# Gating the last weights on GpSimd and closing the last product in two pieces, in a fused two-block transformer kernel

## The reference, cut to what matters

```python
def swiglu(h, w_gate, w_up, w_down):
    return (jax.nn.silu(h @ w_gate) * (h @ w_up)) @ w_down
...
    h = rms_norm(x, g_ffn[l]) * (1.0 + sc_f) + sh_f
    x = x + g_f * swiglu(h, w_ffn_gate[l], w_ffn_up[l], w_ffn_down[l])
    return rms_norm(x, g_final)
```

## Time and profile before

| what | value |
|---|---|
| median of three executions | 961.36 us |
| the profiled execution, its own time | 960.98 us |
| its span, first to last instruction | 959.2 us |
| PE, DVE, ACT, POOL busy | 99%, 72%, 54%, 6% |
| mean granted TensorE clock | 0.997 of full speed |

### The profile page before, as it was taken

The page is one execution under the profiler, slowest core; times in us unless marked ns, Lnnn a source line. Parts: engine busy times, 40 slices in busy tenths (PEclk is TensorE's granted clock), DMA queues, the critical chain, the costliest instruction groups (busy, mean ns, idle before and its releaser), DMA issues.

```text
span 959.2 us, 12959 instructions
## 1 busy us (share of the span) xinstructions
PE 945.3 (99%) x5054; PEld 810.4 (84%) x5054; DVE 685.8 (72%) x932; ACT 518.3 (54%) x732; POOL 54.6 (6%) x96
## 2 busy tenths in 40 slices
PE   8999999999999999999999999998999999999996
PEld 8889888888888888888788888887988888888885
DVE  6956578658888775975788777668678886556555
ACT  6756563536655555264275555547465575444543
POOL 0000121001000002100100000002100000000000
PEclk9999999999999999999999999999999999999998
DMA  9975275527988886183289898764631565655521
GB/s 322 337 253 176 88 268 204 209 88 256 338 278 294 283 295 204 52 314 125 88 317 333 271 306 288 249 221 131 229 132 45 176 225 192 219 176 191 178 71 45
DMA packets 110028, 203.00 MB, mean 212 GB/s; under 512 B 4188, under 2 KB 76144, under 8 KB 106640
## 3 DMA queue, kind: packets, MB, share of 16 engines
q1 hardware_dynamic: 106656, 189.67, 58.4%
q0 software_dynamic: 3168, 12.24, 3.7%
q10 hardware_dynamic: 144, 0.26, 0.1%
HBM read 201.09 MB, written 1.06 MB: 211 GB/s over the span
## 4 chain that ended last, share of the span: by engine, by line
PE 90%; DVE 6%; ACT 2%; issue 1%; POOL 0%; DMA 0%; POOLq 0%; SPq 0%; DVEq 0%; ACTq 0%
PE WB L360 20%; PE YB L385 11%; PE YB L378 10%; PE YB L393 10%; PE WB L363 10%; PE YB L439 4%; PE WB L378 2%; PE WB L342 2%; PE WB L385 2%; PE WB L393 2%; PE WB L349 2%; PE WB L345 2%; PE WB L694 1%; PE WB L713 1%; PE WB L477 1%
## 5 line engine op out<-in xcount | busy, mean ns | idle before, releaser
L1709 DVE TENSOR_TENSOR wl<-raw,wh 128x2048 fp32r<-128x2048 f32 (+1 forms) x146 | 334.3, 2297 | 117.4 <-ACT wh L1101 115.1
L1101 ACT CAST wh<-raw 128x2048 fp32r<-128x2048 f32 (+1 forms) x150 | 285.2, 1905 | 30.5 <-PE YB L439 8.9
L360 PE MATMUL WB<-XS,wh 128*128 128x512 f32 x832 | 208.1, 392 | 0.0
L360 PEld LDWEIGHTS WB<-XS,wh 128*128 128x128 f32 x832 | 152.2, 188 | 29.1
L363 PEld LDWEIGHTS WB<-XS,wl 128*128 128x128 f32 x832 | 113.5, 190 | 8.2
L363 PE MATMUL WB<-XS,wl 128*128 128x256 f32 x832 | 116.0, 282 | 0.0
L378 PE MATMUL YB<-wh,FHT 128*128 128x512 f32 x352 | 109.0, 391 | 0.0
L385 PE MATMUL YB<-wl,FHT 128*128 128x512 f32 x352 | 108.6, 390 | 0.0
L393 PE MATMUL YB<-wh,FLT 128*128 128x512 f32 x352 | 108.5, 389 | 0.0
L1275 ACT COPY U<-WB 128x256 f32<-128x256 f32 x102 | 33.0, 376 | 132.8 <-PE WB L363 132.8
L385 PEld LDWEIGHTS YB<-wl,FHT 128*128 128x128 f32 x352 | 66.1, 188 | 14.1
(11 more groups left out here) (338 smaller groups left out, 1205.2 us busy)
## 6 DMA issues: line engine op xcount, KB each, us to landing
raw<-in_mlp_w SPq DMA_DIRECT2D x64, 1024.0 KB, 5.2
raw<-in_w_ada_t SPq DMA_DIRECT2D x24, 1024.0 KB, 5.1
raw<-in_mlstm_w_in SPq DMA_DIRECT2D x11, 1024.0 KB, 8.0
raw<-in_w_ffn_down SPq DMA_DIRECT2D x11, 1024.0 KB, 4.9
raw<-in_w_ffn_gate SPq DMA_DIRECT2D x10, 1024.0 KB, 5.4
raw<-in_w_ffn_up SPq DMA_DIRECT2D x10, 1024.0 KB, 5.6
raw<-in_mem_w_kv SPq DMA_DIRECT2D x8, 1024.0 KB, 5.1
raw<-in_xattn_wq SPq DMA_DIRECT2D x8, 1024.0 KB, 7.2
```

What stands on the lines that cost most here:

```text
L360: e.matmul(W[:, :], H[:, at(k)], XS[:, k, :], start=k == 0, stop=False)
L1101: f = e.copy(w[:, 0:a * b], raw[:, 0:a * b])
L1709: f = e.tensor_tensor(L[:, 0:a * b], raw[:, 0:a * b], H[:, 0:a * b].bitcast(F32), ALU.subtract)
```

## The change

Three edits go together.

1. POOL multiplies the second 512 columns of both blocks of every down chunk by the gate vector, in place in `raw` (two instructions of 128 x 512 per chunk, 11 chunks). It begins after the norm's last low part (`dve_ln["lo", "ffn", 1, 3]`). ACT's cast of a down chunk waits for POOL and no longer for the landing. DVE then adds the h=1 banks straight to `X`, without the multiplication.
2. The last 512 columns of t=1 come from PE as two pieces: the products of down 9 and 10 for columns 512 to 767 go on in `YB[3]`, those for 768 to 1023 start anew in `YB[0]`. DVE adds all of `YB[3]` to `X` after the first piece and `YB[0]` after the second.
3. ACT squares only columns 512 to 767 of the last half. DVE squares and sums 768 to 1023 itself, adds its sum to POOL's partial one, and makes the last output in one instruction from `X`, the factor and the gain.

```diff
+                        c0, c1 = stops[nb - 1] if nb else 0, stops[nb]
+                        o, start = YB[2 * t + nb] if nb < 2 else apart, (first or nb == 2) and n == 0
+                        if nb == 2 and n == 0:
+                            e.wait_ge(*apart_free)
...
-                    e.wait_ge(*landed(n))
+                    e.wait_ge(*(w_gated[n] if name[0] == "down" else landed(n)))
...
-            for h in range(2):
-                e.wait_ge(*dve_ffn["gated", 1, h])
-                rms_half("out", 1, h)
+            e.wait_ge(*dve_ffn["gated", 1, 0])
+            rms_half("out", 1, 0)
+            e.wait_ge(*dve_ffn["gated", 1, 1])
+            e.activation(JX["out"][1][:, 512:768], X[:, 1, 512:768], ACT.Square, scale=1 / 32,
+                         accum_out=cols(("rms", "out", 1), 6)[:, 1:2]).then_inc(act_ln.add(("ms", "out", 1, 1)))
...
+                if rows == "down" and h == 1:
+                    e.tensor_tensor(X[:, t, cs], X[:, t, cs], YB[2 * t + h][:, :], ALU.add).then_inc(cnt.add(("gated", t, h)))
+                    return
...
+            e.wait_ge(*pe_rows["down", 1, 1])
+            e.tensor_tensor(X[:, 1, 512:1024], X[:, 1, 512:1024], YB[3][:, :], ALU.add).then_inc(dve_ffn.add(("gated", 1, 1)))
             by_g(1, 0)
-            gated("down", dve_ffn, 1, 1, 1)
-            by_g(1, 1)
+            w, last = cols(("rms", "out", 1), 6), X[:, 1, 768:1024]
+            e.wait_ge(*pe_rows["down", 1, 2])
+            e.wait_ge(*dve_ffn["gated", 1, 1])
+            step(e.tensor_tensor(last, last, YB[0][:, 0:256], ALU.add))
+            step(e.scalar_tensor_tensor(U[:, 1, 768:1024], last, 1 / 1024, last, ALU.mult, ALU.mult, accum_out=w[:, 4:5]))
+            e.wait_ge(*po_ln["part", "out", 1])
+            e.tensor_tensor(w[:, 5:6], w[:, 4:5], w[:, 2:3], ALU.add).then_inc(dve_ffn.add("ms"))
             e.wait_ge(*po_ln["r", "out", 1])
-            e.tensor_scalar(U[:, 1, 512:1024], U[:, 1, 512:1024], cols(("rms", "out", 1), 4)[:, 3:4], None, ALU.mult
+            e.scalar_tensor_tensor(U[:, 1, 512:1024], X[:, 1, 512:1024], w[:, 3:4], BV[gi][:, 512:1024], ALU.mult, ALU.mult
...
+            e.wait_ge(*dve_ln["lo", "ffn", 1, 3])
+            for j in range(11):
+                n = N["down", j]
+                r = RAW[n % NR][:, :].rearrange("p (k c) -> p k c", k=2)
+                e.wait_ge(*landed(n))
+                for k in range(2):
+                    f = e.tensor_tensor(r[:, k, 512:1024], r[:, k, 512:1024], GB[:, 1, 512:1024], ALU.mult)
+                f.then_inc(w_gated.add(n))
+            rms_stats("out", (0,))
+            w = cols(("rms", "out", 1), 6)
+            e.wait_ge(*act_ln["ms", "out", 1, 1])
+            e.tensor_scalar(w[:, 2:3], w[:, 1:2], w[:, 0:1], EPS, ALU.add, ALU.add).then_inc(po_ln.add(("part", "out", 1)))
+            e.wait_ge(*dve_ffn["ms"])
+            rsqrt(w[:, 3:4], w[:, 5:6], po_ln.add(("r", "out", 1)))
```

More of the change, by code:

```diff
@@ L305, in build_program @@
         d_bv = [sem(f"in_bv{n}") for n in range(2)]
-        w_hi, w_lo, w_hi0, w_lo0, w_ada, w_pool = (count(n) for n in "w_hi w_lo w_hi0 w_lo0 w_ada w_pool".split())
+        w_hi, w_lo, w_hi0, w_lo0, w_ada, w_pool, w_gated = (
+            count(n) for n in "w_hi w_lo w_hi0 w_lo0 w_ada w_pool w_gated".split())
         pe_turn, pe_front, pe_mlstm, pe_rows, pe_xa, pe_mlp, pe_pool, pe_mix, pe_ffn = (
@@ L399, in tm, with rows @@
                 return parts_[1]()
-            def rows(stage, j, names, xs, first, last, free=None, amid=None, ts=(0, 1)):
+            def rows(stage, j, names, xs, first, last, free=None, amid=None, ts=(0, 1), stops_1=(512, 1024),
+                     apart=None, apart_free=None):
                 ms = [M[n] for n in names]
                 for t in ts:
-                    order = [(nb, n) for nb in range(2) for n in range(len(ms))]
+                    stops = stops_1 if t else (512, 1024)
+                    order = [(nb, n) for nb in range(len(stops)) for n in range(len(ms))]
                     if t == 0:
@@ L414, in rows @@
                             amid()
-                        f = tm(m, 2, 1024, 512 * nb, 512 * nb + 512, YB[2 * t + nb][:, :], t, k0,
-                               first and n == 0, last and n == len(ms) - 1, xh, xl,
+                        c0, c1 = stops[nb - 1] if nb else 0, stops[nb]
+                        o, start = YB[2 * t + nb] if nb < 2 else apart, (first or nb == 2) and n == 0
+                        if nb == 2 and n == 0:
+                            e.wait_ge(*apart_free)
+                        f = tm(m, 2, 1024, c0, c1, o[:, 0:c1 - c0], t, k0,
+                               start, last and n == len(ms) - 1, xh, xl,
                                hi and nb == 0 and (lambda k: hi(t, k)), lo and nb == 0 and (lambda k: lo(t, k)))
@@ L419, in rows @@
                             f.then_inc(pe_rows.add((stage, t, nb)))
-                        elif last and t == nb == 1:
+                        elif last and t == 1 and nb == len(stops) - 1:
                             f.then_inc(pe_rows.add((stage, "end", n)))
@@ L426, in rows @@
                 for n, m in enumerate(ms):
-                    done = (1, 1) if n == len(ms) - 1 else ("end", n)
+                    done = (1, len(stops) - 1) if n == len(ms) - 1 else ("end", n)
                     ends[m] = pe_rows[(stage,) + done if last else (stage, j)]
@@ L1065, in down @@
                        lambda t, k, n=n: hidden(dve_ffn, n, k)) for n in js], js[0] == 0, js[-1] == 10,
-                     free if js[0] == 0 else None)
+                     free if js[0] == 0 else None, stops_1=(512, 768, 1024) if js[-1] == 10 else (512, 1024),
+                     apart=YB[0], apart_free=dve_ffn["gated", 0, 0])
             pair("ffn", [("gate", 0), ("up", 0)], pe_ffn, lambda n: dve_mix["gated", 0, n])
@@ L1401, in rms_half @@
                 cs = slice(512 * h, 512 * h + 512)
-                e.activation(JX[s][t][:, cs], X[:, t, cs], ACT.Square, scale=1 / 32, accum_out=cols(("rms", s, t), 4)[:, h:h + 1]
+                e.activation(JX[s][t][:, cs], X[:, t, cs], ACT.Square, scale=1 / 32, accum_out=cols(("rms", s, t), 6 if s == "out" else 4)[:, h:h + 1]
                              ).then_inc(act_ln.add(("ms", s, t, h)))
@@ L1651, in scalar @@
                 e.copy(FH[0][:, fs], SU[0][:, fs]).then_inc(act_ffn.add(("h", 10, f)))
-            r = [cols(("rms", "out", t), 4)[:, 3:4] for t in range(2)]
+            r = [cols(("rms", "out", t), 6)[:, 3:4] for t in range(2)]
             for h in range(2):
@@ L1664, in scalar @@
             f.then_inc(act_ffn.add(("out", 0)))
-            for h in range(2):
-                e.wait_ge(*dve_ffn["gated", 1, h])
-                rms_half("out", 1, h)
+            e.wait_ge(*dve_ffn["gated", 1, 0])
[3 more added lines that the diff above has]
+                         accum_out=cols(("rms", "out", 1), 6)[:, 1:2]).then_inc(act_ln.add(("ms", "out", 1, 1)))
+            e.wait_ge(*dve_ffn["g", 1, 0])
             e.wait_ge(*po_ln["r", "out", 1])
@@ L2446, in vector @@
             gated("down", dve_ffn, 1, 1, 0)
+            e.wait_ge(*pe_rows["down", 1, 1])
+            e.tensor_tensor(X[:, 1, 512:1024], X[:, 1, 512:1024], YB[3][:, :], ALU.add).then_inc(dve_ffn.add(("gated", 1, 1)))
             by_g(1, 0)
-            gated("down", dve_ffn, 1, 1, 1)
-            by_g(1, 1)
+            w, last = cols(("rms", "out", 1), 6), X[:, 1, 768:1024]
[5 more added lines that the diff above has]
+            e.tensor_tensor(w[:, 5:6], w[:, 4:5], w[:, 2:3], ALU.add).then_inc(dve_ffn.add("ms"))
             e.wait_ge(*po_ln["r", "out", 1])
-            e.wait_ge(*dve_ffn["g", 1, 1])
-            e.tensor_scalar(U[:, 1, 512:1024], U[:, 1, 512:1024], cols(("rms", "out", 1), 4)[:, 3:4], None, ALU.mult
-                            ).then_inc(dve_ffn.add("out"))
+            e.scalar_tensor_tensor(U[:, 1, 512:1024], X[:, 1, 512:1024], w[:, 3:4], BV[gi][:, 512:1024], ALU.mult, ALU.mult
+                                   ).then_inc(dve_ffn.add("out"))
         def gpsimd(e):
@@ L2517, in rms_stats @@
                     e.wait_ge(*act_ln["ms", s, t, 1])
-                    w = cols(("rms", s, t), 4)
+                    w = cols(("rms", s, t), 6 if s == "out" else 4)
                     step(e.tensor_scalar(w[:, 2:3], w[:, 1:2], w[:, 0:1], EPS, ALU.add, ALU.add))
@@ L2577, in gpsimd @@
             bvec("final", I["g_final_2"])
-            rms_stats("out")
+            e.wait_ge(d_gate, 32)
+            e.wait_ge(*dve_ln["lo", "ffn", 1, 3])
[12 more added lines that the diff above has]
+            rsqrt(w[:, 3:4], w[:, 5:6], po_ln.add(("r", "out", 1)))
         def sync(e):
```

## The result

The changed kernel takes 965.53 us (median of 5 executions, 963.05 to 966.01) against 961.36 before. The medians stand 4.2 us apart; the ratio is 1.0038, 95% interval 1.0027 to 1.0049, or +3.7 us (+2.6 to +4.7). This text goes by the ratios, which are not the quotients of two medians. The forecast was 963.4 with a range of 960.9 to 964.6. It is slower by more than was forecast. The profiled execution took 965.53, its span is 963.7.

The account below looks back on a forecast made before the run. The prediction took PE, busy 99% of the span, to bound the kernel. A stall of +3.2 us at the feed-forward entry and -1.2 at the tail made +2.0 on 961.36, so 963.4 us, 8 in 10 range 960.9 to 964.6.

Parts of the forecast that it names:

- What bounds the kernel: Feed-forward stage: PE never idles until its last product, so any wait put on it moves the end by its full length.
- The sum: Whole kernel: entry stall +3.2 and tail -1.2 give +2.0 us on the median 961.36, so 963.4; chance 0.58.
- The turns of POOL and DVE: Feed-forward entry: POOL's multiplications and DVE's low parts alternate, each waiting for the other whole; PE stalls 3.2 us.
- Rivals 1 and 2: Entry: 1, POOL keeps access for both multiplications, stall 1.2, 961.4, chance 0.18; 2, no stall, only the tail, 960.2, 0.12.
- Rival 3: Ahead of down 0: down 1's multiplications meet gate 2's low part, two holds cost another 1.0 us, 964.4; chance 0.09.
- Steady stage: Later down chunks: POOL's gating, 2.4 us a chunk, is hidden by 13 us of slack; price 0.
- The tail: After the last matmul: shorter chain to the power and both outputs starting at once, -1.2 us, between -0.8 and -1.5.

Follow-up runs that it names:

- warm: The changed kernel with 14 throw-away matmuls of 512 columns on PE between gate 1 and the transposes; 963.12 us, ratio 1.0021 against the kernel before.
- pool_early: The changed kernel without POOL's wait for the norm's last low part, so POOL multiplies down 0 earlier; 962.03 us, ratio 1.0008 against the kernel before.
- after_again: The changed kernel as it is, run and profiled once more; 965.55 us, ratio 1.0041 against the kernel before.
- stall_1h: The kernel before, with DVE repeating one and a half low parts of down 0 so that PE waits 2.3 us; ratio 1.0043, +4.1 us.
- stall_2: The kernel before, with DVE repeating the low part of down 0 twice so that PE waits 3.4 us; ratio 1.0057, +5.5 us.

## Why the prediction was wrong

It forecast slower, which was right, and the median lies 0.9 us above its range. Step by step:

- **What bounds the kernel.** "Any wait put on PE in that stage moves the end by its full length, and nothing gives it back." This is the step that failed, and only in its first half. Nothing was given back, but a wait of over two microseconds moved the end by more than its length. The missing term is PE's work at half its clock behind the wait: 1.53 us by the stretch from the transposes to down 0 (1.50 by warm's trace), and 1.7 to 1.9 by the ratios. The sum had it at nothing. With it the sum is +3.5 to +3.9, as measured.
- **The turns of POOL and DVE.** Right in each step (the four rows under the last heading). POOL's first multiplication ended at 780.95, held until DVE's low part had ended; up 1's low part was held in turn and ended at 783.09; POOL's second ended at 784.25. Counted from the first low part, the cast of down 0 was forecast 6.88 later and came 6.77 later; the transposes grew by 3.20, forecast 3.2. Each of POOL's two ended 1.16 us after the low part that held it, 1.20 forecast; without a hold one takes 1.27 to 1.29 (pool_early).
- **Rivals 1 and 2** did not happen. Rival 3, a second stall ahead of down 0, did not either: in that stretch PE has no wait, and the one hold that came (gate 2's low part, 3.05 us rather than 2.29) fits under the 0.9 allowed. The 964.4 that it gave would have been nearer the truth for a wrong reason.
- **Steady stage.** Right: from down 0 to the last matmul +0.13, of which the 24 short matmuls were forecast to take 0.12. The ten later chunks cost nothing, with POOL's pairs stretched to about 4 us each.
- **The tail.** The forecast's -1.2 holds the +0.12 of the short matmuls; counted alike, the traces give -1.13. The power starts 1.20 us after the last matmul's end, forecast 1.24, though the terms listed there add up to 1.28. So this part gained 1.47, forecast 1.43, and the outputs gave back 0.21 of it rather than 0.1: the last one is issued 1.41 us after the power rather than 1.35 and lands 2.7 us after its issue rather than 2.5.
- **The clock** stood in the profile before all along: PE is busy without a gap from 785.2 on and the clock is full, so no row of before shows what a gap of three microseconds does in that place. The forecast had a bound for the length of the wait, and none for what follows it. The Trainium skill (TensorE: Matmul & The Clock Gate, The HAM clock gate) says that the halved rate is the resting state and that activity releases it; the traces agree: 0.50 at or behind the waits of 2.3 to 3.4 us, and 1.00 again after PE had worked for 3.2 to 5.9 us.

## What to carry to other kernels

Where one queue serves both a prefetch and the chain that PE waits for, an added wait on the prefetch belongs behind the chain's instructions: moving down 0's cast and low part (and with them gate 2's) turned +3.7 us into -1.4. A wait of PE is priced by its length only while it is short; measured here, 1.1 us cost 1.2, 2.3 cost 4.1 (but 2.0 in one of five executions) and 3.4 cost 5.5. Other work for PE in the wait kept the clock at full (warm). And idle POOL is not free for two-operand work: each of its multiplications and those of DVE's instructions that read both operands from SBUF waited for one another whole, so look for the one place where DVE is on the path.

## What the hardware showed that I had not expected

- The granted clock in stretches of half a microsecond: after the changed kernel's wait of 3.06 us it was 0.50 from 789.1, 0.2 before PE went on, for 3.4 us; in after_again likewise. In stall_1h it fell 0.3 us after PE had gone on from its wait of 2.34, and stayed for 3.4. In stall_2, with a wait of 3.39, it fell 1.0 before PE went on and stayed for 6.8. In these four executions the low stretch is not set by the wait's length alone.
- Instructions of POOL and DVE with both operands in SBUF took strict turns. The timeline of the changed kernel in short windows, where the pairs above come apart:

```profile
777.51 2.28 DVE L1721 TENSOR_TENSOR wl<-raw,wh 128x2048 fp32r<-128x2048 f32 x1
...
777.74 3.21 POOL L2606 TENSOR_TENSOR raw<-raw,AR 128x512 f32<-128x512 f32 x1 [3.35 <-issue]
...
779.71 3.38 DVE L1721 TENSOR_TENSOR wl<-raw,wh 128x2048 fp32r<-128x2048 f32 x1
...
780.91 3.34 POOL L2606 TENSOR_TENSOR raw<-raw,AR 128x512 f32<-128x512 f32 x1
```

  Each is on record from its issue, so the ends tell the order: 779.79, 780.95, 783.09, 784.25. But DVE's cast from one operand, issued at 775.07 while POOL's first was running, waited for POOL's second too, 2.50 us for a 0.29 us instruction. A waiting DVE instruction is not always let in between two of POOL's. Which property of the cast makes the difference was not tried.
